# Moving columns read and results written in alternating runs instead of straight through

## The reference, cut to what matters

```python
z = jnp.einsum('bsd,dc->bsc', h, w_in[l])                 # block 1: 10248 columns
cb, cc, cv, q, k, v, f_logit, gate_c, gate_a = jnp.split(z, SPLIT_POINTS, axis=-1)
conv_y = cb * causal_dwconv(cc * cv, conv_w[l])
conv_branch = jnp.einsum('bsc,cd->bsd', conv_y, w_conv_out[l])
attn_branch = jnp.einsum('bsc,cd->bsd', attn, w_attn_out[l])
merged = gc * conv_branch + ga * attn_branch
x = x + jnp.einsum('bsd,de->bse', merged, w_mix_out[l])
u = jnp.square(jax.nn.relu(jnp.einsum('bsd,df->bsf', h, w_ff1[l])))   # 8192 columns
x = x + jnp.einsum('bsf,fd->bsd', u, w_ff2[l])
...
mix = jnp.concatenate([attn, ssm], axis=-1) @ w_out[l]    # block 2
x = x + gate_m * mix
x = x + gate_f * conv_ffn(h, w_up[l], conv_ffn_w[l], conv_ffn_b[l], w_down[l])
```

## Time and profile before

| | |
|---|---|
| median of the timed runs | 2517.05 us |
| span of the profiled execution | 2514.4 us |
| TensorE busy | 2491.9 us, 14373 matmuls |
| VectorE busy | 1972.6 us |
| ScalarE busy | 1266.1 us |
| GpSimd busy | 91.9 us |
| DMA | 567.01 MB, mean 226 GB/s |

### The profile page before, as it was taken

One profiled execution on the slowest core, in us unless ns is written; L12 is line 12 of the kernel. 1 busy time (PEld: TensorE's weight loads), 2 busy tenths in 40 slices (PEclk: granted clock), 3 DMA queues, 4 the chain that ended last, 5 costly groups with the idle time before them and its releaser, 6 DMA issues.

```text
span 2514.4 us, 46915 instructions
## 1 busy us (share of the span) xinstructions
PE 2491.9 (99%) x14373; PEld 2166.9 (86%) x14373; DVE 1972.6 (78%) x3113; ACT 1266.1 (50%) x2038; POOL 91.9 (4%) x109
## 2 busy tenths in 40 slices
PE   8999999999999999999999999999999999999998
PEld 7888888888888888888888888888888888888887
DVE  7778776689887887887888877776886886886886
ACT  5344445565554454443555555564544444445455
POOL 0000001000000000000000114300000000000000
PEclk9999999999999999999999999999999999999999
DMA  7786785557888888888888555545556556556554
GB/s 276 267 275 204 272 274 183 196 188 259 280 280 286 278 281 284 277 285 281 277 283 275 169 175 189 185 164 186 166 178 190 195 179 193 192 171 208 185 171 162
DMA packets 162668, 567.01 MB, mean 226 GB/s; under 512 B 18867, under 2 KB 19180, under 8 KB 162604
## 3 DMA queue, kind: packets, MB, share of 16 engines
q1 hardware_dynamic: 132428, 458.91, 54.7%
q10 hardware_dynamic: 27792, 101.20, 12.2%
q0 software_dynamic: 2384, 6.09, 1.0%
HBM read 563.70 MB, written 2.42 MB: 225 GB/s over the span
## 4 chain that ended last, share of the span: by engine, by line
PE 82%; DVE 1%; ACT 1%; issue 0%; DVEq 0%; POOL 0%; ACTq 0%; POOLq 0%
PE bank L301 82%; DVE w_lo L1305 0%; ACT w_hi L788 0%; DVE scratch L1338 0%; PE bank L643 0%; PE bank L511 0%; DVE Z L2008 0%; ACT G L1117 0%; DVE scratch L1816 0%; PE bank L588 0%; DVE G L1788 0%; DVE scratch L1704 0%; PE bank L502 0%; ACT L1117 0%; ACT L827 0%
## 5 line engine op out<-in xcount | busy, mean ns | idle before, releaser
L301 PE MATMUL bank<-H,w_hi 128*128 128x512 f32 (+1 forms) x4480 | 1409.8, 394 | 11.5 <-DVE w_lo L1367 9.5
L1305 DVE TENSOR_TENSOR w_lo<-w_raw,w_hi 128x1024 fp32r<-128x1024 f32 (+2 forms) x898 | 1048.6, 1177 | 127.5 <-ACT w_hi L788 117.4
L301 PEld LDWEIGHTS bank<-H,w_lo 128*128 128x128 f32 x4416 | 830.7, 188 | 190.8
L788 ACT ACTIVATE w_hi<-w_raw 128x1024 fp32r<-128x1024 f32 (+2 forms) x898 | 876.3, 1013 | 16.4 <-PE bank L301 8.2
L301 PE MATMUL bank<-H,w_lo 128*128 128x256 f32 x4416 | 871.5, 278 | 0.0
L301 PEld LDWEIGHTS bank<-H,w_hi 128*128 128x128 f32 x4480 | 688.8, 189 | 17.5 <-issue 14.3
L301 PE MATMUL bank<-U,w_hi 128*128 128x512 f32 (+1 forms) x2011 | 626.8, 392 | 0.0
L818 ACT ACTIVATE scratch<-bank 128x256 f32<-128x256 f32 x355 | 136.4, 384 | 743.2 <-PE bank L301 742.9
L301 PEld LDWEIGHTS bank<-U,w_lo 128*128 128x128 f32 x1984 | 371.7, 188 | 85.3
L301 PE MATMUL bank<-U,w_lo 128*128 128x256 f32 x1984 | 401.7, 281 | 0.0
L301 PEld LDWEIGHTS bank<-U,w_hi 128*128 128x128 f32 x2011 | 311.3, 188 | 2.9 <-DVE w_lo L1305 0.2
(11 more groups left out here) (243 smaller groups left out, 1118.0 us busy)
## 6 DMA issues: line engine op xcount, KB each, us to landing
w_raw<-in_w_ff SPq DMA_DIRECT2D x256, 512.0 KB, 5.1
ada_w<-in_w_ada ACTq DMA_DIRECT2D x192, 512.0 KB, 4.6
w_raw<-in_w_up SPq DMA_DIRECT2D x176, 512.0 KB, 3.9
w_raw<-in_w_z SPq DMA_DIRECT2D x96, 512.0 KB, 5.0
w_raw<-in_w_in SPq DMA_DIRECT2D x88, 512.0 KB, 4.2
w_raw<-in_w_gate SPq DMA_DIRECT2D x64, 512.0 KB, 4.6
w_raw<-in_w_down SPq DMA_DIRECT2D x64, 384.0 KB, 3.1
w_raw<-in_w_down SPq DMA_DIRECT2D x64, 320.0 KB, 3.3
```

Source lines behind the costliest of these rows:

```text
L301: return nc.tensor.matmul(out, lhsT, rhs, start=start, stop=stop, skip_group_check=True)
L788: A(w_hi[:, slot, 0:cols], w_raw[:, slot, 0:cols], ACT.Copy).then_inc(sem("w_high"), 1)
L1305: TT(w_lo[:, slot, 0:cols], w_raw[:, slot, 0:cols], w_hi[:, slot, 0:cols].bitcast(F32), ALU.subtract)\
```

## The change

A third and a fourth argument of a unit, `run` and `low_run`, give the moving operand and the output of `high` and `low` another order of columns. `in_runs` cuts the columns into two halves and each half into runs of `run` columns; the address pattern then goes: first run of the left half, first run of the right half, second run of the left half, and so on. Operand and output have the same order, so each column's result lands where it did before. The number of columns, of matmuls, of weight loads and of waits is what it was; a value of 0 leaves the pattern as it was.

Seven loops get values: gate (run 4), conv_in (2), conv_mul and v (8, low 4), qk (16, low 8), branch (32, low 16), mix (64, low 64) and ff1 in all four groups (128, low 32). gate2, ff2, everything of the second block, and the pairs with code of their own stay as they were.

```diff
+            def in_runs(ap, run):
+                return ap.rearrange("p (s l j) -> p l s j", s=2, j=run) if run else ap
...
                     def high(c):
                         start = c == 0 and (h == 0 or two_banks)
-                        return mm(dst[:, :], w_hi[:, 2 * par + h, c * P:(c + 1) * P], buf[:, k0 + c, :], start, False)
+                        return mm(in_runs(dst[:, :], run), w_hi[:, 2 * par + h, c * P:(c + 1) * P],
+                                  in_runs(buf[:, k0 + c, :], run), start, False)
...
-                        return mm(dst[:, T:2 * T], w_lo[:, 2 * par + h, c * P:(c + 1) * P], buf[:, k0 + c, 0:T], False, stop)
+                        return mm(in_runs(dst[:, T:2 * T], low_run), w_lo[:, 2 * par + h, c * P:(c + 1) * P],
+                                  in_runs(buf[:, k0 + c, 0:T], low_run), False, stop)
...
             with pe.Fori(2, 8) as i:
-                pair_of_units(PAIR0["gate"] + i, H, NC)
+                pair_of_units(PAIR0["gate"] + i, H, NC, run=4)
...
             with pe.Fori(1, 8) as i:
-                pair_of_units(PAIR0["conv_in"] + i, H, NC)
+                pair_of_units(PAIR0["conv_in"] + i, H, NC, run=2)
...
             with pe.Fori(0, 8) as i:
-                pair_of_units(PAIR0["conv_mul"] + i, H, NC)
+                pair_of_units(PAIR0["conv_mul"] + i, H, NC, run=8, low_run=4)
             with pe.Fori(0, 7) as i:
-                pair_of_units(PAIR0["qk"] + i, H, NC)
+                pair_of_units(PAIR0["qk"] + i, H, NC, run=16, low_run=8)
...
             with pe.Fori(1, 8) as i:
-                pair_of_units(PAIR0["branch"] + i, B, NC, two_banks=True)
+                pair_of_units(PAIR0["branch"] + i, B, NC, two_banks=True, run=32, low_run=16)
...
             with pe.Fori(1, 8) as i:
-                pair_of_units(PAIR0["mix"] + i, U, NC)
+                pair_of_units(PAIR0["mix"] + i, U, NC, run=64, low_run=64)
...
             def ff1(g, first=0):
                 with pe.Fori(first, 8) as i:
-                    pair_of_units(PAIR0["ff"] + 16 * g + i, H, NC)
+                    pair_of_units(PAIR0["ff"] + 16 * g + i, H, NC, run=128, low_run=32)
```

More of the change, by code:

```diff
@@ L306, in keep_warm, with unit @@
                     mm(bank[5][:, :], wn[:, 0:P], wn[:, :], True, True)
-            def unit(pair, par, buf, chunks, operand=None, operand_base=0, two_banks=False, between=None, fresh=False):
+            def in_runs(ap, run):
+                return ap.rearrange("p (s l j) -> p l s j", s=2, j=run) if run else ap
+            def unit(pair, par, buf, chunks, operand=None, operand_base=0, two_banks=False, between=None, fresh=False,
+                     run=0, low_run=0):
                 cut = FIRST_CHUNKS if chunks == NC else (chunks + 1) // 2
```

## The result

The changed kernel took 2555.3 us (2555.13 to 2555.47, two runs) against 2517.05 us: ratio 1.0153, 95% interval 1.0123 to 1.0182, 38 us slower. That is within 2%, but it is clear of the measurement's uncertainty, and the forecast was that nothing would be paid. It lies inside the predicted range only because the range left room for rivals A and B; the forecast's own range, 2512 to 2526, doesn't hold it.

A forecast was written before the change was run, and what follows sets the result against it. The prediction took TensorE's matmul pace to bound the kernel: 2514.4 us + 0 for all jumps, and with the 2.7 us by which timed runs exceed the span, 2517 us. The range was 2508 to 2590 us.

The forecast's parts named there:

- Rival A: conv_in's runs of 2 stream at half pace because operand portions exceed 8 bytes: 52 us, 2569 us; chance 0.09.
- Rival B: All seven loops: one column lost per jump, in proportion to the runs, 68 us, 2586 us; chance 0.09.
- What bounds the kernel: Whole kernel: every stage runs at the pace at which TensorE starts matmuls; TensorE is busy 99% of the span.
- The step that failed: All seven loops: jumps between runs cost 0, inferred from the free jump between two matmuls.
- The counting: Seven loops: 73 changed pairs and 150,784 runs, 57,344 of them in conv_in.
- Accumulation: Additions to one output column stay 256 to 512 columns apart; the shortest distance is the old one.
- C: Every split pattern is slow: 764 us paid again, 3281 us, or 2703 us with a threshold; chance 0.08.
- D: The new order lifts the steady stream's extra 8 to 9%: 61 us faster, 2456 us; chance 0.05.
- The rule and the rows: Rows say jumps cost nothing; the skill calls non-contiguous patterns slow; its 16-byte lines suggest 4 us for runs of 2.

The follow-up runs named there:

- e1: The changed kernel with only the moving operand read in the new order and the output written straight, against the kernel before: 2554.3 us, ratio 1.0147.
- e2: The changed kernel with only the output written in the new order and the moving operand read straight, against the kernel before: 2516.7 us, ratio 0.9996.
- e12: Kernel before with every ordinary unit reordered on both sides, runs of 8 in 4 passes for tile H, runs of 4 for U and B: 2481.5 us, ratio 0.9855.
- e3: The changed kernel's run lengths, but all even runs first and then all odd ones, against the kernel before: 2572.5 us, ratio 1.022.

## Why the prediction was wrong

**What bounds the kernel: right, but for a few pairs.** TensorE's pace sets the end; what each matmul took longer came out at the end. The exception is that VectorE set the pace in some pairs of conv_mul (0.8 us before), so the prediction was wrong to say that nothing covers TensorE there, and mix isn't the stage in which VectorE is nearest to its limit: from 246 to 258 us it is busy 11.33 of 12.

**The step that failed** is "A jump in both addresses thus costs nothing that a difference of 3 ns could show. I take that: 0 for all 150,784." The term of the sum that was wrong is this zero: the runs measured 38 us in its place, paid wholly on the reading side (e1 and e2).
**The counting was right**: 73 pairs and 150,784 runs, of which conv_in's 38% cost 59%. **Accumulation** played no part (e2).

**Rival A** (half pace for runs of 2) named the right side and the right place, but not the price: 22.8 us instead of 52 with halves 1 KB apart. Its half pace appeared at strides of 16 and 32 bytes (0.45 us a `high`). It also expected nothing from longer runs, which cost 16 us. **Rival B** had the right shape for 4 to 16 columns, at less than half its price. **C** fell: in the change's orders 2 columns in a row are enough for writes, and for reads the runs of 64, and of 128 with 32, cost nothing. **D**'s 61 us are not reached, but e12's 35.5 us come from where D looked, by other orders than the change's.

**The rule and the rows.** In e2 writing runs of 2 to 128 columns changed the time by a factor of 0.9996. The Trainium skill's "Any non-contiguous AP significantly slows down matmuls" ("Advanced Engine Details and Errata", PSUM Cachelines) is not borne out for these. In e3 16-byte portions used half at each visit took 0.445 us a `high`, and portions used whole left gate's pairs at 11.25 us. The Trainium skill's "Advanced Engine Details and Errata", SBUF Cachelines, gives lines of 16 bytes, which this agrees with. It also asks for at least two hits per line, which runs of 2 have. For these 4-byte columns at the upper level of the clock that was not enough: 0.445 us against 0.2325.

**What stays open:** why alternating runs of 2 cost 1.3 ns a visit and not 1.8; why a stride of 256 bytes is the worst and 64, or 128 with 32-byte runs, the best; and what chooses among the paces of one order.

## What to carry to other kernels

In this kernel, whose moving operand has 4-byte columns, a matmul at the upper level of the clock is bound by the reading of that operand (0.2325 us for 512 columns, where one order of reading took 0.215). So short runs that alternate between two halves cost at once on the reading side (0.2 ns a run, 0.4 if each takes only half of 16 bytes), while the order of the output was free where it was tried alone. Runs of 64 columns, and of 128 with 32, alternated at no cost; other orders with long runs did cost, such as runs of 32 in 4 passes (11.31 us against 11.24). And when a row bounds the cost of something rare, its uncertainty must be multiplied by the new count before the cost is called zero.

## What the runs showed that was not expected

The straight order is not the fastest. Runs of 8 columns taken every 128 bytes in 4 passes gave 10.88 us a pair against 11.15, and runs of 4 every 64 bytes 11.01 against 11.24 (both sides reordered), while twice those strides lost 5% (11.73 with runs of 8 every 256 bytes, 11.68 with runs of 4 every 128). Which order is best differs between tiles (with U and B, runs of 8 in 4 passes took 11.28), and one order has several steady paces, 10.88, 10.99 and 11.20 us, in loops of identical instructions; the change's own runs of 4 have two, 11.73 and 11.95.
